# Second PEER layer of a transformer kernel: 128 of 512 tokens by gathered rows of a copied table, 384 tokens by dense matmuls, low weight parts on DVE

## What is computed

```
q = x @ wq                                   # 8 heads, 2 halves of 128
s = q . sub_keys                             # 128 scores per head and half; the 16 best of each half
experts[h, 0:16] = a * 128 + b               # the 16 best pairs (a, b) of a head, out of 128 * 128 = 16384 experts
g = softmax(best scores)                     # 16 gates per head
act = gelu(expert_u[experts] . x)            # first expert layer, (16384, 1024)
y = sum over heads and picks of (g * act) * expert_v[experts]      # second expert layer, (16384, 1024)
```

## Time and profile before

| | us |
|---|---|
| median of 3 runs | 3104.93 |
| lowest and highest run | 3100.42, 3110.15 |
| span of the profiled execution (its own time; no other is listed for it) | 3119.8 |
| PE busy in it | 3027.5 (97%) |
| DVE busy | 1790.2 (57%) |
| POOL busy | 1547.0 (50%) |
| ACT busy | 928.5 (30%) |
| mean share of the 16 DMA engines in use | 38% |

### The profile page before, as it was taken

How to read it: one execution, slowest core, us unless ns; L and a number is a source line. 1 busy time by engine, 2 the same in 40 slices (tenths; PEclk the granted TensorE clock), 3 DMA queues, 4 the chain that set the end, 5 groups by cost and what they waited for, 6 DMA issues and landing times.

```text
span 3119.8 us, 40047 instructions
## 1 busy us (share of the span) xinstructions
PE 3027.5 (97%) x15372; PEld 1965.7 (63%) x15516; DVE 1790.2 (57%) x3290; ACT 928.5 (30%) x1472; POOL 1547.0 (50%) x788
## 2 busy tenths in 40 slices
PE   8999999899999999998999999999999999999998
PEld 6888686688667887886778444455545444444444
DVE  6433398635653433014621999689995456655564
ACT  2001214623661012114222322343333332223222
POOL 5664268955015666466456443345644333443342
PEclk9998799999999999999999999999999999999999
DMA  3222122122332223222122434355555765556551
GB/s 146 108 81 96 44 108 71 26 97 71 132 139 108 108 85 125 95 81 102 55 108 101 183 139 157 149 229 216 202 202 228 243 215 203 191 198 215 208 193 57
DMA packets 139991, 429.99 MB, mean 138 GB/s; under 512 B 8800, under 2 KB 79584, under 8 KB 116704
## 3 DMA queue, kind: packets, MB, share of 16 engines
q1 hardware_dynamic: 125376, 353.40, 31.8%
q10 hardware_dynamic: 7200, 68.68, 5.3%
q0 software_dynamic: 7296, 6.31, 0.9%
HBM read 358.10 MB, written 73.40 MB: 138 GB/s over the span
## 4 chain that ended last, share of the span: by engine, by line
PE 86%; POOL 5%; DVE 4%; issue 3%; DMA 1%; ACT 1%; SPq 0%; DVEq 0%; ACTq 0%; POOLq 0%
PE bank L1140 13%; PE bank L1141 13%; PE bank L1142 13%; PE bank L691 4%; PE bank L692 3%; PE bank L694 3%; POOL rpb_tiles L2459 3%; PE bank L952 3%; PE bank L947 3%; PE bank L948 3%; PE bank L721 3%; PE bank L722 2%; PE bank L749 2%; PE bank L726 2%; PE bank L743 2%
## 5 line engine op out<-in xcount | busy, mean ns | idle before, releaser
L2504 POOL TENSOR_TENSOR work<-ring,work 128x4096 bf16<-128x4096 f32 x64 | 582.8, 9106 | 791.7 <-ACT work L1589 791.7
L1140 PE MATMUL bank<-work 128*128 128x512 bf16 x2005 | 761.1, 380 | 5.7 <-DVE work L2345 2.7
L1141 PE MATMUL bank<-work 128*128 128x512 bf16 x2005 | 761.4, 380 | 3.3 <-ACT work L1600 1.0
L1142 PE MATMUL bank<-work 128*128 128x512 bf16 x1990 | 755.6, 380 | 2.3
L2528 POOL CAST w_parts<-ring 128x1024 fp32r<-128x1024 f32 (+3 forms) x212 | 231.6, 1092 | 652.9 <-DMA ring<-in_wstream 150.6
L2530 POOL TENSOR_TENSOR w_parts<-ring,w_parts 128x1024 fp32r<-128x1024 f32 (+3 forms) x212 | 511.5, 2413 | 17.0
L2345 DVE TENSOR_TENSOR work<-hF,work 128x512 bf16<-128x512 f32 x128 | 307.8, 2405 | 252.5 <-ACT work L1674 249.4
L1142 PEld LDWEIGHTS bank<-work 128*128 128x128 bf16 x2048 | 200.6, 98 | 242.4 <-issue 1.4
L1140 PEld LDWEIGHTS bank<-work 128*128 128x128 bf16 x2048 | 200.7, 98 | 238.7 <-issue 4.7
L1141 PEld LDWEIGHTS bank<-work 128*128 128x128 bf16 x2048 | 200.6, 98 | 234.6 <-issue 1.4
L2313 DVE SCALAR_TENSOR_TENSOR work<-const,work 128x256 f16<-128x256 f32 x512 | 299.1, 655 | 30.0 <-PE bank L1164 29.8
(11 more groups left out here) (424 smaller groups left out, 4942.2 us busy)
## 6 DMA issues: line engine op xcount, KB each, us to landing
ring<-in_wstream SPq DMA_DIRECT2D x128, 2048.0 KB, 7.7
hidden<-hF ACTq DMA_DIRECT2D x32, 1024.0 KB, 3.9
gates<-work ACTq DMA_DIRECT2D x16, 2048.0 KB, 8.8
hF<-hidden SPq DMA_DIRECT2D x32, 1024.0 KB, 7.1
work<-gates SPq DMA_DIRECT2D x32, 1024.0 KB, 10.2
rpb_tiles<-in_rpb POOLq DMA_DIRECT2D x192, 16.0 KB, 2.3
work<-rpb_tiles POOLq DMA_DIRECT2D x24, 128.0 KB, 4.4
ring<-in_wstream SPq DMA_DIRECT2D x5, 512.0 KB, 4.0
```

Source lines behind the costliest of these rows:

```text
L1140: pe.matmul(out, a(0), b(0), start=(start and k == 0), stop=False)
L1141: pe.matmul(out, a(0), b(1), start=False, stop=False)
L1142: mm = pe.matmul(out, a(1), b(0), start=False, stop=(stop and k == n - 1))
L2504: nc.gpsimd.tensor_tensor(SPLIT[:, p, 1, :], ring[:, p, :], SPLIT[:, p, 0, :], ALU.subtract).then_inc(lo, 1)
```

## The change

Tokens 0 to 127 leave the dense second layer and the dense gate table. While the first 64 weight loads run, SP also copies all of `expert_v` in DRAM into a table of plain rows, `expert_rows` (64 DMAs of 1 MB, written in pieces of 512 bytes). Once the hidden stage is over, POOL issues 128 indirect DMAs that fetch, for each of the 128 tokens, its hidden value of pick s (4 bytes each), and then 128 indirect DMAs that fetch the row of `expert_v` of pick s (128 rows of 4 KB, 512 KB each) into eight buffers. DVE multiplies each by its weight and adds it to `PICK_SUM`, spread over slots 6 to 31 of the outputs stage; at the end PE transposes that sum into the banks. The other 384 tokens go through the dense layer as before, in matmuls of 384 columns. The low part of the `expert_v` weights moves from POOL to DVE, between the four multiplies and the four low products. The weights of a slot are loaded from `expert_rows` (pieces of 4 KB). `hidden` is stored in pieces of 2 KB, and only 384 tokens of it are read back. The gate table has 12 chunks in slots 14 to 25. Some semaphores are used a second time in place of new ones (`REUSED`, `since`).

```diff
@@ constants
-        GATE_FROM, GATE_TO = 14, 30
+        PICKED = P
+        DENSE = S - PICKED
+        GATE_FROM = 14
+        GATE_TO = GATE_FROM + DENSE // GT
+        expert_rows = nc.dram_tensor("expert_rows", (N_KEYS * N_KEYS, D), f32, kind="Internal").ap()
+        PICKS = PEER_HEADS * 16
+        PICK_BATCH = 64
+        PICK_FROM = 6
+        PICK_BUF = [area(12288 + 1024 * b, D) for b in range(4)] + [area(28800 + 1024 * b, D) for b in range(4)]
@@ sync engine
+            def copy_rows(n):
+                q, k, r = n // (2 * KT), n // 2 % KT, n % 2 * (ROWS_Q // 2)
+                rows_ = expert_rows.rearrange("(r p) d -> p r d", p=P)[:, q * ROWS_Q + r:q * ROWS_Q + r + ROWS_Q // 2, :]
+                sp.dma_start(rows_[:, :, k * P:(k + 1) * P],
+                             wstream[peer + 16 * q + 8 + k].rearrange("p (r j) -> p r j", j=P)[:, r:r + ROWS_Q // 2, :])\
+                    .then_inc(signal("experts_copied"), 16)
...
                 sp.dma_start(ring[:, n % 2, 0:k], wstream[FIRST[name] + m][:, 0:k]).then_inc(slot_full[n % 2], 16)
+                if n <= 2 * QUARTERS * KT:
+                    copy_rows(n - 1)
...
-                sp.wait_ge(slot_used[p], (peer + s) // 2)
+                if v < 2:
+                    sp.wait_ge(slot_used[p], (peer + s) // 2)
+                else:
+                    sp.wait_ge(signal("v_split"), v - 1)
...
-                    sp.dma_start(ring[:, p, :].rearrange("p (k n) -> p k n", k=KT),
-                                 wstream[at:at + KT].rearrange("k p n -> p k n")[:, :, v % 8 * 512:v % 8 * 512 + 512])\
+                    sp.dma_start(ring[:, p, :].rearrange("p (r d) -> p r d", r=ROWS_S),
+                                 expert_rows[512 * v:512 * v + 512].rearrange("(r p) d -> p r d", p=P))\
@@ tensor engine, outputs
-                            mm = products(bank[:, k, :], [pair(p, r, k)], opening, False)
+                            mm = products(bank[:, k, PICKED:S], [pair(p, r, k)], opening, False)
...
-                    products(bank[:, k, :], [pair(1, r, k) for r in range(ROWS_S)], False).then_inc(summed, 1)
+                    products(bank[:, k, PICKED:S], [pair(1, r, k) for r in range(ROWS_S)], False)
+                    if k == 0:
+                        pe.wait_ge(signal("gathered"), PICKS + 1)
+                    pe.transpose(bank[:, k, 0:PICKED], PICK_SUM[:, k * P:(k + 1) * P], ident).then_inc(summed, 1)
@@ vector engine, outputs
+                def pick(n):
+                    b = n % len(PICK_BUF)
+                    dve.wait_ge(signal(f"picked_in{b}"), since(f"picked_in{b}", 16 * (n // len(PICK_BUF) + 1)))
+                    dve.wait_ge(gathered, n + 1)
+                    v.scalar_tensor_tensor(out=PICK_SUM, in0=PICK_BUF[b], scalar=PICK_W[:, n:n + 1], in1=PICK_SUM,
+                                           op0=ALU.mult, op1=ALU.add).then_inc(gathered, 1)
+                n = 0
+                for s in range(U_SLOTS):
+                    i, p = s // 2, s % 2
+                    dve.wait_ge(gates_in[p], 16 * i + 16)
+                    dve.wait_ge(hidden_in[p], 16 * i + 16)
+                    for j in range(ROWS_S):
+                        h = hF[:, 4 * p + j, PICKED:S].rearrange("p (c t) -> p c t", t=GT)
+                        v.tensor_tensor(h, h, G_IN[:, p, :, j, :], ALU.mult).then_inc(w_made, 1)
+                    dve.wait_ge(signal("split_hi"), U_SLOTS + s + 1)
+                    v.tensor_tensor(SPLIT[:, p, 1, :], ring[:, p, :], SPLIT[:, p, 0, :], ALU.subtract)\
+                        .then_inc(signal("v_split"), 1)
+                    for j in range(ROWS_S):
+                        dve.wait_ge(w_hi, 4 * s + j + 1)
+                        v.tensor_tensor(W[:, 4 * p + j, 1, :], hF[:, 4 * p + j, PICKED:S], W[:, 4 * p + j, 0, :],
+                                        ALU.subtract).then_inc(w_lo, 1)
+                    if s == PICK_FROM:
+                        for b in range(PICKS // PICK_BATCH):
+                            batch = slice(b * PICK_BATCH, (b + 1) * PICK_BATCH)
+                            dve.wait_ge(signal(f"units_in{b}"), since(f"units_in{b}", 16 * PICK_BATCH))
+                            ins = v.tensor_tensor(PICK_W[:, batch], PICK_W[:, batch], PICK_GATE[:, batch], ALU.mult)
+                        order(ins)
+                    while s >= PICK_FROM and n < PICKS * (s + 1 - PICK_FROM) // (U_SLOTS - PICK_FROM):
+                        pick(n)
+                        n += 1
@@ gpsimd
-                with pool.Fori(0, U_SLOTS) as i:
+                with pool.Fori(0, U_SLOTS // 2) as i:
...
+            def gather():
+                def units(n):
+                    for s in range(n * PICK_BATCH, (n + 1) * PICK_BATCH):
+                        pool.indirect_dma_start(PICK_W[:, s:s + 1], None, hidden_of,
+                                                bass.IndirectOffsetOnAxis(PICK_UNIT[:, s:s + 1], 0))\
+                            .then_inc(signal(f"units_in{n}"), 16)
+                def expert(s):
+                    if s >= len(PICK_BUF):
+                        pool.wait_ge(signal("gathered"), s - len(PICK_BUF) + 2)
+                    pool.indirect_dma_start(PICK_BUF[s % len(PICK_BUF)], None, expert_rows,
+                                            bass.IndirectOffsetOnAxis(PICK_ROW[:, s:s + 1], 0))\
+                        .then_inc(signal(f"picked_in{s % len(PICK_BUF)}"), 16)
+                pool.wait_ge(signal("picked"), since("picked", 1))
+                pool.wait_ge(signal("experts_copied"), 2 * QUARTERS * KT * 16)
+                for p in range(2):
+                    pool.wait_ge(signal(f"spilled{p}"), U_SLOTS // 2 * 16)
+                    pool.wait_ge(signal(f"split_used{p}"), U_SLOTS // 2)
+                for n in range(PICKS // PICK_BATCH):
+                    units(n)
+                for s in range(PICKS):
+                    expert(s)
```

More of the change, by code:

```diff
@@ L222, in build, with since @@
         sems = {}
+        REUSED = {name: ("idx_rotated", 1 + n) for n, name in
+                  enumerate(("lat_scaled", "vn_centred", "vn_ready", "r_shifted", "r_chosen", "picked"))}
+        REUSED.update({name: ("lat_sq", 1 + n) for n, name in enumerate(("ctx_root", "vn_root", "r_exp"))})
+        REUSED.update({"n_mask_in": ("x_in0", 16), "n_rows_out": ("x_in1", 16), "n_first_windows_in": ("opening_in", 16),
+                       "n_windows_in": ("rows_in", 48), "units_in0": ("n_rpb_arranged", 192 * 16)})
+        REUSED.update({f"picked_in{b}": (f"n_rpb_in{b}", 96) for b in range(4)})
+        def since(name, n):
+            return REUSED[name][1] + n if name in REUSED else n
         def signal(name):
+            if name in REUSED:
+                name = REUSED[name][0]
             if name not in sems:
@@ L519, in _ @@
                 if (name, m) == ("d_pb", 0):
-                    sp.wait_ge(signal("n_rows_out"), 16)
+                    sp.wait_ge(signal("n_rows_out"), since("n_rows_out", 16))
                     sp.wait_ge(signal("parts_used"), CHUNK["d_pa"])
@@ L869, in latents @@
                 turned = signal("lat_turned")
-                pe.wait_ge(signal("lat_scaled"), 1)
+                pe.wait_ge(signal("lat_scaled"), since("lat_scaled", 1))
                 for k in range(5):
@@ L1050, in spatial @@
                 pe.wait_ge(signal("ctx_and_ws_in"), 32)
-                pe.wait_ge(ready, 1)
+                pe.wait_ge(ready, since("vn_ready", 1))
                 for g in range(GROUPS):
@@ L1129, in turn_choices @@
                 turned = signal("choice_turned")
-                pe.wait_ge(signal("r_chosen"), 1)
+                pe.wait_ge(signal("r_chosen"), since("r_chosen", 1))
                 for c in range(3):
-                    for t in range(NT):
+                    for t in range(PICKED // P, NT):
                         mm = pe.transpose(bank[:, 4 + c, t * P:(t + 1) * P], R_E[:, t, c, :], ident)
@@ L1266, in _ @@
             conv_in("a_in1", "a1")
-            project_out("a_out1", rest, y_rest, [("conv_convolved", 15), ("ctx_root", 1)], norm_context)
+            project_out("a_out1", rest, y_rest, [("conv_convolved", 15), ("ctx_root", since("ctx_root", 1))], norm_context)
             norm("d1")
@@ L1504, in spread @@
             def spread():
-                act.wait_ge(signal("vn_centred"), 1)
+                act.wait_ge(signal("vn_centred"), since("vn_centred", 1))
                 for t in range(NT):
@@ L1652, in hidden_units @@
                     both(i)
-                act.wait_ge(signal("r_shifted"), 1)
+                act.wait_ge(signal("r_shifted"), since("r_shifted", 1))
                 act.activation(R_BV, R_BV, ACT.Exp).then_inc(signal("r_exp"), 1)
@@ L1657, in hidden_units @@
                     act.wait_ge(signal("choice_turned"), c + 1)
-                    act.activation(E_T[:, c, :], bank[:, 4 + c, :], ACT.Copy).then_inc(signal("choice_moved"), 1)
```

(23 more changed lines are left out.)

80 lines of the change are left out of this document (37 added, 43 removed).

## The result

The changed kernel takes 3051.2 us (median of 4 runs, 3049.9 to 3070.4) against 3105.9 before: a ratio of 0.983, 95% interval 0.980 to 0.986, so 1.7% shorter. The forecast was 3038 us.

A forecast was written before the change was run, and what follows sets the result against it. The prediction took PE to bound both expert stages; terms -16.3 - 36.3 + 56.8 - 83.0 + 6.7 + 5 = -67.1 took 3104.9 to 3038 us, with 2925 to 3150 us as its 8-in-10 range.

The forecast's parts named there:

- gates of 12 slots: Hidden stage: four slots lose their gates and fall from 24.8 to 20.7 us; -16.3 us.
- slots 0 to 6 at 15.54 us: Outputs stage before the picks weigh: PE sets the pace with 384-column matmuls, 5.18 us less a slot; -36.3 us.
- wait for the single values: Start of slot 7: PE stalls behind DVE, which waits for POOL's 128 single-value DMAs; +56.8 us.
- slots 7 to 31 at 17.4 us: Outputs stage with picks: DMA sets the pace, 6.25 MB a slot at 360 GB/s; -83.0 us, ends -129.5 and -60.5.
- the end: Last slot: PE waits 4.5 us for the last picks and eight transposes add 2.2; +6.7 us.
- the copy: SP's queue: 64 copy DMAs between weight loads, mostly hidden; +5 us, ends 0 and 70.
- c: POOL's issue time for one indirect DMA, taken as 1.14 us; forecast wrong if under 0.8 or above 1.4.
- 129c - 90.3: Formula for PE's stall before slot 7 in us: zero up to c = 0.70, 168 at c = 2.
- Rival B: DVE holds up POOL's single-value issue: c 2.0, stall 168 us, pick slots 18.3 us; 3171 us, slower; chance 0.17.
- Rival A: Outputs stage all hidden: c 0.7 or less, DMA at 400 GB/s, no stall, slots 15.54 us; 2930 us; chance 0.17.
- C: Slots 7 to 31: transfers get no more than 302 GB/s, slots take 20.7 us; 3121 us; chance 0.12.
- D: Copies make weight loads late in the tight places, +50 instead of +5 us; 3083 us; chance 0.10.

The follow-up runs named there:

- run 2: Kernel before with only the copy of expert_v added, 64 DMAs of 1 MB behind the first 64 weight loads, table unused; 3106.7 us, ratio 1.000.
- run 4: Changed kernel with picks starting at slot 12 in place of 6; 3017.4 us, ratio 0.969.
- run 6: Changed kernel with only every second gather of rows, each buffer added twice with two weights; 3031.1 us, ratio 0.976.
- run 9: Changed kernel, nothing left out: single values in batches of 32, first batch ahead, then one after each gather of rows; picks from slot 5; 2973.3 us, ratio 0.955.
- run 5: Changed kernel without DVE's adds of the picks, all 256 indirect DMAs kept; 3040.8 us, ratio 0.980.
- run 3: Changed kernel without the picks: no indirect DMAs of rows or values, no adds; 2926.9 us, ratio 0.942.
- run 11: Changed kernel with DVE's low part of 4096 elements made in four instructions of 1024; 3040.0 us, ratio 0.978.
- run 1: Kernel before with only the low part of the second layer's weights moved to DVE; 3107.2 us, ratio 1.000.
- run 10: Changed kernel, nothing left out: single values in batches of 32, first batch ahead, then one after each gather of rows; picks from slot 4; 2963.8 us, ratio 0.954.

## Why the prediction was right, point by point

The sum against the parts measured in the trace of after (and in the runs):

| step | predicted | measured |
|---|---|---|
| gates of 12 slots | -16.3 | hidden stage 730.0 to 716.7 us: -13.3 |
| slots 0 to 6 at 15.54 us | -36.3 | 110.9 in place of 146.7: -35.8 |
| wait for the single values | +56.8 | +96.2 |
| slots 7 to 31 at 17.4 us | -83.0 | 408.9 in place of 518.0: -109.1 |
| the end | +6.7 | last slot 24.1 in place of 15.6 (before 20.9 in place of 20.7), the rest 0.2 longer: +8.5 |
| the copy | +5 | run 2: 0 |
| sum | -67.1 | -53.5 |

3104.9 - 53.5 = 3051.4, and 3051.2 was measured. The two profiles differ by more, 69.3 us. 15.7 of it lie before the first expert product (1711.9 against 1696.2 us), and they are no gain of the change: in the profiled executions of before and of runs 4, 6 and 9 the granted clock is at its lower level, 1.2 GHz, for 34 us from about 348 us on, and there the first product comes at 1712 to 1716 us; in the ten other executions, which lack this stretch, it comes at 1690 to 1702.

**What is luck in it.** The total missed by 13.6 us, but its two large terms missed by more, in opposite directions: the stall by +39.4 us, the slots behind it by -26.1. With only the slots put right the sum would have said 3012, with only the stall 3077. The prediction also named its own sign of being wrong, "if c is under 0.8 or above 1.4". c was 1.45, so by that sign this step failed in its size; the slots (16.4 us, between 16 and 18.5) passed. That the total lies near the forecast shows the parts to be the right ones, and not their sizes.

**Gates.** A slot with gates takes 24.29 us in both kernels, except slot 25, with 30.5 us before and 31.3 after (its cause was not traced). The mean of 24.8 held a share of this one slot, which four gate slots fewer do not save.

**The wait.** The mechanism and its formula, 129c - 90.3, held: c was (2600.8 - 2416.4)/127 = 1.45 us, which gives 96.8. What was mis-sized is c, "nearest to the dear end: I take c = 1.14". An indirect DMA takes 0.94 us of POOL and 0.30 us between two, so 1.25 alone (59 of them in 2527 to 2600 us, where DVE stands still); beside DVE's work 1.47 + 0.30 (the first 49, to 2503 us). The mean duration, 1.15 us with DVE's holds in it, met my 1.14; the gap between two, which I had left out, is the whole of the miss.

**Slots with picks.** The step "I take 360 GB/s, 17.4 us" was too dear. With always busy engines and 4 KB rows they move 386 GB/s, near the 391 of the earlier trace rows, so 16.2 us a slot; measured 16.4. The bound itself was named rightly (runs 5 and 6 and the waits of after), and DVE stayed under PE as worked out: 4.42, 1.28 and 0.56 us were met within 0.01.

**The end.** PE's wait for the last adds is 4.5 us, as worked out. In it, at 3018.7 us, the granted clock falls to 1.2 GHz and stays there to 3025.5, which the prediction had put at nothing. The transposes cost less than forecast: the last slot of run 3, with the same eight and no wait, takes 16.5 us, 0.9 above the pace. So 7.5 us are the wait with the low clock behind it. **The copy** cost nothing (run 2), where I had taken 5.

**Rival B** described half of what happened. Its place was right: DVE's two-tensor instructions hold up POOL's indirect DMAs (run 11 shows it: 4.99 us beside the long instruction, 1.97 beside short ones). Its price was not: one DMA per long DVE instruction waits, and others beside the short products take 1.10 in place of 0.94 us, so the pitch rose to 1.77 us and not to 2.0, and during the stall DVE stood still and POOL ran free. My case against B did not hold: the descriptors' writing was held for a whole instruction, and the 24 issues of the earlier trace rows were no test, since DVE is busy only 55.9 of the 278 us around them and has no instruction of 4 us there. The Trainium skill says in GPSIMD Engine Reference, Key points, that GpSimd's SBUF interfaces are shared with VectorE and collide with instructions that have two SBUF inputs, and in DMA: Bandwidth & Descriptors, SWDGE vs HWDGE vs iDMA, that GpSimd's descriptors go into SBUF. By these two the trace agrees, now for GpSimd's DMAs too: 4.99 us in place of 0.94. That it takes two inputs in SBUF no run here shows, for none tries a long instruction with one.

**Rival A** failed on c, since 1.25 us is the pitch even beside an idle DVE, and at 386 GB/s the slots would have stayed above 15.6 us. **C** and **D** fell: 386 GB/s, and run 2. The move of the low part cost nothing (run 1), as forecast.

## What to carry to other kernels

A queue of many small indirect DMAs is priced by the issuing engine, pitch (duration and gap) times count, and what stands behind the last of them in someone's program order pays for all; interleave them with the work they feed, in batches just large enough. Where POOL issues DMAs beside a busy DVE, short DVE instructions let it through (run 11). When an engine other than the bound is at 95% of a slot, count on slots above the bound's own pace (runs 9 and 10). When a forecast of several terms comes close, hold each term against the trace before you trust the method.

## What was not expected of the hardware

- An indirect DMA of 128 single values of 4 bytes and one of 128 rows of 4 KB cost POOL the same, 0.94 and 0.93 us at the least; the rows take longer to land, 9.9 us in the median against 2.4.
- Between two indirect DMAs POOL shows 0.30 us for which the trace has no releaser, 39 us for 128 of them.
- A copy of 1 MB in DRAM in pieces of 512 bytes lands in 10.3 us, and 64 of them hid between the weight loads (run 2), even where these are some 8 us apart.
- In the stall PE's granted clock fell to its lower level (at 2527.2 us) and came back only after PE had worked again, at 2622.8, 2.8 us into slot 7 (0.57 of full over 2610 to 2625 us); that cost 1.4 us, slot 7 taking 16.96 us in place of 15.60.
